# Forget rows and state-space rows fetched by DMA broadcast instead of by matrix products, the time steps computed beside the first merge, token blocks weighed together

## Chip, cores and metric

The kernel runs on one core of a Trainium2 chip. The metric is the device time of one execution in microseconds (us). A core has TensorE (PE, matrix products into eight PSUM banks), VectorE (DVE), ScalarE (ACT), GpSimd (POOL) and SyncE (SP). Nearly all DMAs of this kernel are issued from SP's program, in its order, so a wait in it holds back every transfer behind it.

## The reference, cut to what matters

The program computes two transformer-like blocks over 512 tokens of width 1024. The change touches the mixer of the first block: attention with a forget gate, and a state-space mixer (SSM) with 32 heads.

```python
proj = h @ w_in
q, k, v, f_raw, u_pool, z, xbc, dt_raw, gate_raw = split_columns(proj)
log_f = jax.nn.log_sigmoid(f_raw.astype(jnp.float32) + b_forget)     # 16 heads
...
F = jnp.transpose(jnp.cumsum(log_f, axis=1), (0, 2, 1))
logits = einsum(q, k) * scale + F[:, :, s0:s1, None] - F[:, :, None, :s1]
p = jax.nn.softmax(jnp.where(mask, logits, -jnp.inf), axis=-1)       # causal, blocks of 128 queries
...
dt = jax.nn.softplus(dt_raw.astype(f32) + dt_bias)                   # 32 heads
a = -jnp.exp(a_log.astype(f32))
a_cs = jnp.cumsum(dt * a, axis=2)                                    # within a chunk
seg = a_cs[:, :, :, None] - a_cs[:, :, None, :]
decay = jnp.where(causal, jnp.exp(jnp.where(causal, seg, 0.0)), 0.0)
scores = cb[..., None] * decay * dt[:, :, None]
y_diag = einsum(scores, xs);  y_off = einsum(cm, h_prev) * jnp.exp(a_cs)
y = (y_diag + y_off + d_skip * xs) * jax.nn.silu(z)                  # then an RMS norm by group
merged = gates[0] * y_att + gates[1] * y_pool + gates[2] * y_ssm
```

The term of F at the query drops out of the softmax, so the kernel needs only the row of F over the keys, the same for every query, which means the same on all 128 partitions.

## The kernel before

The mixer runs in stages with a barrier between them: opening (0 to 60 us), attention, first merge, pool, SSM, second merge. Inside a stage every engine follows its own program, and semaphores tie them. Products with fp32 weights are done in three passes: a weight is split by ACT (`high`) and DVE (`low`) into two fp32r parts, and PE multiplies high by high, high by low and low by high. A tile of 128 output columns is thus 24 matmuls of 512 columns.

**Opening.** The last product (L326) gives the raw forget gates, 128 columns of `w_in` of which 16 are used, and the first pair's queries.

**Attention** (`attention_stage`). Eight head pairs i, four query blocks b of 128. In a step (i, b) PE issues `scores(i, b+1)`, half a projection of the next pair (12 matmuls, L840), `turn` (transposes of the probabilities, L878), the other half, and `weigh` (L890). `scores` first spreads the forget row of each of the two heads over the partitions by two matmuls (L861: a picked column of 16 rows, broadcast, times the high and low part of F, at least 256 columns wide), then adds the products of queries and keys (L865). DVE takes `row_max` (L1034, adding `wide_mask`), `normalise`, the `low` parts of later weights, and six to eight steps of a matrix-vector product for the second block (`matvec`, L1067 and L1069), whose 1 MB strips SP loads into three slots. ACT does the exponents (L963) and the copies.

**First merge** (`merge_stage`, branch 0). Eight halves of weights, 48 matmuls each, on PE (L543); ACT and DVE prepare the next half (L517, L521) and apply the gate.

**SSM** (`ssm_stage`). First tiles: one for the 32 raw time steps (`dt`), then six of group 0, which pass a convolution (`conv` on DVE, L1578 and L1580) and an activation (tanh on ACT, `silu` on DVE, L1596). Between them DVE computes the time steps, softplus and the running sums `acs` (`raw_times` to `sums`, L1621 to L1650). `turn_small` needs them. Then for each of four groups i: tiles of the next group and gate tiles at ten places (`tile_at(i, 0)` to `(i, 9)`), `turn_x` for four token blocks (L1297), on DVE `weigh` for each (L1670, L1675), `chunk_products` (L1304), `state` (L1315), then four head pairs f: `rows` (L1330: each head's row of `acs` spread over the partitions by two matmuls of 512 columns), `exponents` on ACT (L1478 to L1482), `scores` on DVE (L1700, L1702), `heads` on PE (L1345, L1349), `outputs` on DVE (L1707, L1709), `square` on ACT.

The order of work is written out by hand; the lines below set it around the change. `more(i, n)` names the tile at place n of group i; `tile(t)` on DVE forms what is due of the earlier tiles and then makes the low part of tile t+2, and on ACT it waits for tile t before it makes the high part of tile t+2.

## Time and profile before

| | us |
|---|---|
| median of three runs | 2770.69 |
| the runs | 2768.95 to 2771.82 |
| profiled execution | 2773.53 |
| its span, first to last instruction | 2771.7 |
| PE busy in the span | 2518.8 (91%) |
| DVE busy | 1763.2 (64%) |
| ACT busy | 1132.4 (41%) |
| mean granted TensorE clock | 0.941 |

The span lacks 1.8 us of the execution's own time. Busy times of a stage are read from stretches cut at the barriers: attention from 59.7 to 338.6 us, the first merge to 433.9, SSM from 538.5 to 907.2. A matmul of 512 columns shows a duration of 0.39 us, but the next starts some 0.24 us after it, so the cost of products is read from start to start.

### The profile page before, as it was taken

To read this page: it belongs to the slowest core of one execution; us is meant where nothing else is said; L and a number is where in the kernel's file an instruction comes from. 1 tells how busy PE (TensorE), PEld (TensorE's weight loads), DVE (VectorE), ACT (ScalarE), POOL (GpSimd) and SP (SyncE) were. 2 spreads that over 40 slices of the span, in tenths; PEclk is the share of its full clock that TensorE was granted. 3 is DMA by queue.
4 is the path that set the end of the run, shared out by engine and by line. 5 is a ranking of instruction groups with operands and counts; after the bars stand their busy time and mean duration, and the time that the engine had idled before them with its cause. 6 is when DMAs were issued, how large, how long until landed. Compare 5 with 4: busy or idle time off the path is not lost. (4 is left out here: it accounts for less than half of the span.)

```text
span 2771.7 us, 32845 instructions
## 1 busy us (share of the span) xinstructions
PE 2518.8 (91%) x12831; PEld 1984.4 (72%) x12831; DVE 1763.2 (64%) x2557; ACT 1132.4 (41%) x1635; POOL 45.1 (2%) x153
## 2 busy tenths in 40 slices
PE   7999799989999989599993898899997979899998
PEld 6666487677777777388882356688886977688886
DVE  5888724486776675689984465677766573642434
ACT  4444322135545324478873243531324144441323
POOL 0000001000000000100001000000000000000000
PEclk8999799999999998599996999999998889999998
DMA  6776637122221843699983112224333314223221
GB/s 232 237 236 227 215 126 273 54 76 61 69 54 61 306 149 76 247 376 417 418 353 151 50 50 69 76 99 152 111 102 108 87 25 167 76 96 102 91 92 31
DMA packets 293562, 415.68 MB, mean 150 GB/s; under 512 B 24906, under 2 KB 212797, under 8 KB 283552
## 3 DMA queue, kind: packets, MB, share of 16 engines
q1 hardware_dynamic: 285568, 383.69, 40.8%
q0 software_dynamic: 5392, 20.97, 1.9%
...
## 5 line engine op out<-in xcount | busy, mean ns | idle before, releaser
L3597 PE MATMUL banks<-big,late_parts 128*128 128x512 f32 x1920 | 443.4, 393 | 11.1 <-DVE late_parts L3770 7.3
L3597 PEld LDWEIGHTS banks<-big,late_parts 128*128 128x128 f32 x1920 | 363.5, 189 | 89.4 <-DVE late_parts L3770 7.5
L3597 PE MATMUL banks<-h_parts_second,late_parts 128*128 128x512 f32 x1440 | 332.6, 391 | 12.8 <-DVE h_parts_second L3794 12.8
L3597 PEld LDWEIGHTS banks<-h_parts_second,late_parts 128*128 128x128 f32 x1440 | 272.0, 189 | 70.9 <-issue 14.4
L3770 DVE TENSOR_TENSOR late_parts<-w_second,late_parts 128x2048 fp32r<-128x2048 f32 x69 | 158.1, 2292 | 218.8 <-ACT late_parts L3659 218.7
L2300 DVE TENSOR_TENSOR expert_parts<-w,expert_parts 128x2048 fp32r<-128x2048 f32 x102 | 233.1, 2289 | 29.1 <-ACT expert_parts L2296 28.7
L1270 PE MATMUL banks<-h_parts,ssm_parts 128*128 128x512 f32 x984 | 239.8, 401 | 6.6 <-DVE ssm_parts L1566 6.1
L3659 ACT ACTIVATE late_parts<-w_second 128x2048 fp32r<-128x2048 f32 x69 | 132.0, 1914 | 256.1 <-PE banks L3597 256.1
L1270 PEld LDWEIGHTS banks<-h_parts,ssm_parts 128*128 128x128 f32 x984 | 186.6, 192 | 53.9 <-DVE ssm_parts L1566 7.9
L2296 ACT ACTIVATE expert_parts<-w 128x2048 fp32r<-128x2048 f32 x102 | 194.7, 1916 | 64.1 <-PE banks L2307 64.1
L2307 PE MATMUL banks<-expert_parts,expert_xt 128*128 128x512 f32 x816 | 195.2, 399 | 6.0 <-DVE expert_xt L2824 6.0
L2307 PEld LDWEIGHTS banks<-expert_parts,expert_xt 128*128 128x128 f32 x816 | 155.8, 193 | 39.4 <-DVE expert_xt L2824 6.9
L543 PE MATMUL banks<-h_parts,front_parts 128*128 128x512 f32 x576 | 135.5, 398 | 8.6 <-DVE front_parts L521 6.5
L840 PE MATMUL banks<-h_parts,qkv_parts 128*128 128x512 f32 x552 | 139.2, 402 | 3.4 <-SPq L158 3.4
L543 PEld LDWEIGHTS banks<-h_parts,front_parts 128*128 128x128 f32 x576 | 110.3, 192 | 33.4 <-DVE front_parts L521 6.8
L1069 DVE SCALAR_TENSOR_TENSOR attention_mod_sum<-w,silu_c,attention_mod_sum 128x512 f32<-128x512 f32 x168 | 126.1, 751 | 5.1
L840 PEld LDWEIGHTS banks<-h_parts,qkv_parts 128*128 128x128 f32 x552 | 101.5, 190 | 35.3 <-issue 11.4
L3682 ACT ACTIVATE tail_r<-banks,cols 128x512 f32<-128x512 f32 x64 | 40.5, 685 | 201.3 <-PE banks L3597 201.3
L543 PE MATMUL banks<-h_parts,ssm_parts 128*128 128x512 f32 x480 | 111.5, 394 | 6.0 <-DVE h_parts L1941 3.1
L3803 DVE TENSOR_TENSOR tail_q<-tail_r 128x512 f32<-128x512 f32 x64 | 41.4, 688 | 114.3 <-ACT tail_r L3682 114.2
L543 PEld LDWEIGHTS banks<-h_parts,ssm_parts 128*128 128x128 f32 x480 | 91.0, 190 | 26.2 <-issue 3.9
L2307 PE MATMUL banks<-expert_parts,expert_ht 128*128 128x512 f32 x408 | 99.2, 400 | 4.5 <-DVE expert_ht L2829 4.5
...
## 6 DMA issues: line engine op xcount, KB each, us to landing
...
```

The source lines that it names most:

```text
L543: mm = pe.matmul(out, self.parts[:, n % 2, w, kk, f * P:(f + 1) * P], x[:, v, kk, :], start=(start and kk == 0 and j == 0), stop=(stop and ...
L840: mm = pe.matmul(ps[:, bank, :], parts[:, j, w, kk, :], k.hp[:, x, kk, :], start=(kk == 0 and n == 0), stop=(kk == KD - 1 and n == 2))
L1069: ins = dve.scalar_tensor_tensor(out=acc, in0=w, scalar=by, in1=acc, op0=ALU.mult, op1=ALU.add)
L1270: mm = pe.matmul(ps[:, t % 2, :], parts[:, t % SPLITS, w, kk, :], k.hp[:, x, kk, :], start=(kk == 0 and j == 0), stop=(kk == KD - 1 and j ...
L2296: act.activation(self.high_part(h), self.raw(h), ACT.Copy).then_inc(self.high_done, 1)
L2300: dve.tensor_tensor(self.low_part(h), self.raw(h), self.high_part(h).bitcast(F32), ALU.subtract).then_inc(self.low_done, 1)
L2307: mm = pe.matmul(out, x[:, v, first + kk, :], self.tile(h, w, kk), start=(start and kk == 0 and j == 0), stop=(stop and kk == KE - 1 and j ...
L3597: mm = pe.matmul(ps[:, bank(n, f), :], w_part(n, w)[:, kk, f * P:(f + 1) * P], x[:, v, kk, :], start=(first_chunk(n) and kk == 0 and j == ...
L3659: act.activation(w_part(n, 0), raw_half(k, n), ACT.Copy).then_inc(s["high_done"], 1)
L3682: act.activation(r[:, c % 2, :], ps[:, bank(n, c % HT), :], ACT.Relu, bias=k.cols[:, b1 + at:b1 + at + 1]).then_inc(s["relu_done"], 1)
L3770: dve.tensor_tensor(w_part(n, 1), raw_half(k, n), w_part(n, 0).bitcast(F32), ALU.subtract).then_inc(s["low_done"], 1)
L3803: dve.tensor_tensor(q[:, c % 2, :], r[:, c % 2, :], r[:, c % 2, :], ALU.mult).then_inc(s["squared"], 1)
```

## The change

**Forget row in attention.** `F` is no longer spread by PE. DVE forms the running sum (without the sign change), SP stores it to DRAM (`forget_store`, 16 rows) and loads each pair's two rows by a broadcast over 128 partitions into `f_rows` (512 KB, two slots). `row_max` adds this row instead of `wide_mask`, and PE adds the causal mask of the diagonal block by one 128-column product of an identity (`eye`) with `mask` for each head.

**Time steps.** The forget gate's product takes 32 columns of the forget gates and 32 of the time steps (64 instead of 128 weight columns, two DMAs of 128-byte runs). ACT copies the raw time steps out of PSUM and SP stores them. The whole chain up to `acs` stands in the first merge (`time_steps(n)` behind half n), and its results go through DRAM to the SSM stage, whose `dt` tile, chain and parts of `acs` are gone. `chunk_ends` stays there.

**SSM rows.** `rows` on PE is gone. SP loads the row of `acs` of each head by broadcast (256 KB) into one of four buffers, two heads at a time, when the exponents two pairs before are done. `exponents` reads them from SBUF. On DVE `weigh` runs for all four token blocks before the next convolution is formed, and `outputs(i, f-1)` stands ahead of `scores(i, f+1)`. At the stage's end the two halves of one product change places.

```diff
+    k.dt_store, k.dt_raw = (k.nc.dram_tensor(name, (G_SSM * R_SSM, T), F32, kind="Internal").ap() for name in ("dt_store", "dt_raw"))
+    k.acs_store = k.nc.dram_tensor("acs_store", (G_SSM * R_SSM, T), F32, kind="Internal").ap()
...
+            sp.dma_start(f_raw[:, :, 0:DT_ROW], columns(w_in, F0, DT_ROW)).then_inc(s["forget_loaded"], 16)
+            sp.dma_start(f_raw[:, :, DT_ROW:], columns(w_in, DT0, GATED - DT_ROW)).then_inc(s["forget_loaded"], 16)
...
+                        mm = pe.matmul(ps[0:n, bank, :], w[:, a, kk, :], k.hp[:, v, kk, :], start=(kk == 0 and j == 0),
...
+                src = k.forget_store[2 * i:2 * i + 2, :].rearrange("(o h) t -> o h t", o=1).to_broadcast([P, 2, T])
+                sp.dma_start(f_rows[:, i % 2], src).then_inc(s[f"f_loaded{i % 2}"], 16)
...
+            sp.wait_ge(s["dt_copied"], 1)
+            sp.dma_start(k.dt_raw, dt).then_inc(s["dt_stored"], 16)
+            sp.wait_ge(s["f_summed"], 1)
+            sp.dma_start(k.forget_store, f_sum).then_inc(s["f_stored"], 16)
+            sp.wait_ge(s["f_stored"], 16)
+            load_forget(0)
+            load_forget(1)
...
+                    if i >= 1 and i + 1 < pairs and j == MOD_SLOTS:
+                        sp.wait_ge(s["max_done"], UNITS * i)
+                        load_forget(i + 1)
...
+                    pe.matmul(ps[:, unit % 4, 0:n], qt[rows, i % 2, b * P:n], kt[rows, i % 2, 0:n], start=True, stop=False)
...
-                    for x in range(2):
-                        pe.matmul(ps[:, unit % 4, 0:wide], pick[:, 2 * i + hh:2 * i + hh + 1].to_broadcast([HEADS, P]),
-                                  f_parts[:, x, 0:wide], start=(x == 0), stop=False)
...
+                    pe.matmul(ps[:, unit % 4, b * P:n], eye[:], mask[:], start=False, stop=True).then_inc(s["scores_done"], 1)
...
+            act.activation(eye[:], k.ident[:], ACT.Copy).then_inc(s["mask_ready"], 1)
+            act.activation(mask[:], k.future_mask[:], ACT.Copy, scale=-1.0).then_inc(s["mask_ready"], 1)
+            act.activation(dt, ps[DT_ROW:GATED, 0, :], ACT.Copy).then_inc(s["dt_copied"], 1)
...
+                    if b == 0 and hh == 0:
+                        dve.wait_ge(s[f"f_loaded{i % 2}"], 16 * (i // 2 + 1))
                     dve.wait_ge(s["scores_done"], unit + 1)
-                    dve.tensor_tensor_reduce(out=ps[:, unit % 4, 0:n], in0=ps[:, unit % 4, 0:n], in1=wide_mask[:, T - n:T], scale=1.0,
+                    dve.tensor_tensor_reduce(out=ps[:, unit % 4, 0:n], in0=ps[:, unit % 4, 0:n], in1=f_rows[:, i % 2, hh, 0:n], scale=1.0,
...
-            dve.wait_ge(s["f_high"], 1)
-            dve.tensor_tensor(f_parts[:, 1], neg_f, f_parts[:, 0].bitcast(F32), ALU.subtract).then_inc(s["f_ready"], 1)
...
+            dve.tensor_tensor_scan(f_sum, ones, f_ln, 0.0, ALU.mult, ALU.add).then_inc(s["f_summed"], 1)
...
-    tiles = [("dt", 0, 0)] + [("conv", 0, c) for c in range(NC_SSM)]
+    tiles = [("conv", 0, c) for c in range(NC_SSM)]
...
+        row = sb("row", [P, DEEP - 1, T])
+        row = [row[:, h, :] for h in range(DEEP - 1)] + [flat[:, 3 * KD * STRIP - T:]]
...
+            def tiles_to(t):
+                while RAWS + loaded.at < min(t, TILES):
+                    sp.wait_ge(s["w_low"], loaded.at + 1)
+                    load_ssm(k, sp, RAWS + loaded.take())
+
+            def load_rows(n):
+                for head in (2 * n, 2 * n + 1):
+                    sp.dma_start(row[head % DEEP], k.acs_store[head:head + 1, :].to_broadcast([P, T])).then_inc(s[f"row_loaded{head % DEEP}"], 16)
+
+            sp.dma_start(dt, k.dt_store).then_inc(s["small_loaded"], 16)
+            sp.dma_start(acs, k.acs_store).then_inc(s["small_loaded"], 16)
+            tiles_to(FIRST + 2)
+            load_rows(0)
+            load_rows(1)
+            for i in range(G_SSM):
+                if i + 1 == G_SSM:
+                    tiles_to(TILES)
+                    sp.wait_ge(s["w_low"], TILES)
+                    halves.load(sp, base)
+                    halves.load(sp, base + 1)
+                for f in range(KG):
+                    n = KG * i + f
+                    if i + 1 < G_SSM:
+                        tiles_to(more(i, 3 + f) + 7)
+                    if n + 2 < KG * G_SSM:
+                        sp.wait_ge(s["seg_done"], 2 * n + 2)
+                        sp.wait_ge(s["row_exp"], 2 * n + 2)
+                        load_rows(n + 2)
...
+                pe.wait_ge(s["acs_ready"], TB)
...
-            def rows(i, f):
...
-                    for x in range(2):
-                        mm = pe.matmul(ps[:, 4 + h % 2, :], pick[:, head:head + 1].to_broadcast([NH, P]), acs_parts[:, x, :],
-                                       start=(x == 0), stop=(x == 1))
-                    mm.then_inc(s["row_done"], 1)
...
+                    if f == 0 and i == 0:
+                        pe.wait_ge(s["decay_done"], 2)
+                    elif f == 0:
+                        pe.wait_ge(s["std_done"], i)
...
+                    act.wait_ge(s[f"row_loaded{h % DEEP}"], 16 * (head // DEEP + 1))
                     if head >= DEEP:
...
+                        ins = act.activation(seg[:, h % DEEP, mine], row[h % DEEP][:, mine], ACT.Abs, bias=small[1][:, c, head:head + 1])
                     ins.then_inc(s["seg_done"], 1)
...
-                weigh(i, 0)
-                weigh(i, 1)
+                for c in range(TB):
+                    weigh(i, c)
                 if more(i, 2) is not None:
                     form(more(i, 2))
-                weigh(i, 2)
...
                         follow(TILES)
+                    if f >= 1:
+                        outputs(i, f - 1)
                     if f + 1 < KG:
                         scores(i, f + 1)
                     if i + 1 == G_SSM and f in (0, 3):
                         halves.low(dve, base + f // 3)
-                    if f >= 1:
-                        outputs(i, f - 1)
...
+                sp.wait_ge(s["dt_summed"], 1)
+                sp.dma_start(k.dt_store, dt).then_inc(s["dt_out"], 16)
+                sp.dma_start(k.acs_store, acs).then_inc(s["dt_out"], 16)
+                sp.wait_ge(s["dt_out"], 32)
...
+                    act.wait_ge(k.small_loaded, 32)
+                    act.activation(k.a_log[:], k.a_log[:], ACT.Exp).then_inc(s["dt_act"], 1)
+                    act.wait_ge(s["dt_step"], 3)
+                    act.activation(e, e, ACT.Exp).then_inc(s["dt_act"], 1)
+                if not last and n == 1:
+                    act.wait_ge(s["dt_step"], 4)
+                    act.activation(t2, t1, ACT.Ln).then_inc(s["dt_act"], 1)
...
+            def time_steps(n):
+                if n == 0:
+                    dve.wait_ge(s["dt_loaded"], 16)
+                    dve.wait_ge(k.small_loaded, 32)
+                    dt_step(dve.memset(ones, 1.0))
+                    dt_step(dve.tensor_scalar(dt, dt, k.dt_bias[:], None, ALU.add))
+                    dt_step(dve.scalar_tensor_tensor(out=e, in0=dt, scalar=-1.0, in1=dt, op0=ALU.mult, op1=ALU.min))
+                elif n == 1:
...
+                    dt_step(dve.tensor_tensor(t1, t1, acs, ALU.add))
+                    dt_step(dve.tensor_tensor(t2, t2, acs, ALU.add))
...
+                    for c in range(TB):
+                        mine = slice(c * P, (c + 1) * P)
+                        ins = dve.tensor_tensor_scan(acs[:, mine], ones[:, mine], t1[:, mine], 0.0, ALU.mult, ALU.add)
+                    ins.then_inc(s["dt_summed"], 1)
```

PE's program in attention, around the widest step of the first pair. `attention_pick` and `attention_f_parts` are the spread forget row, `attention_eye` and `attention_mask` the mask product; "x4" counts two heads and two parts. Before:

```order
L890 MATMUL banks<-merged,attention_v 64x128 x4
L861 MATMUL banks<-attention_f_parts,attention_pick 128x512 x4
L865 MATMUL banks<-attention_kt,attention_qt 128x512 x2
L840 MATMUL banks<-h_parts,qkv_parts 128x512 x12
L878 MATMUL banks<-ident,merged 128x128 x6
L840 MATMUL banks<-h_parts,qkv_parts 128x512 x12
```

After:

```order
L915 MATMUL banks<-merged,attention_v 64x128 x4
L888 MATMUL banks<-attention_kt,attention_qt 128x512 x2
L891 MATMUL banks<-attention_mask,attention_eye 128x128 x2
L869 MATMUL banks<-h_parts,qkv_parts 128x512 x12
L903 MATMUL banks<-ident,merged 128x128 x6
L869 MATMUL banks<-h_parts,qkv_parts 128x512 x12
```

The four row products ahead of the scores are gone, and two narrow products stand behind them.

PE's program in SSM, from the stage's start to the first heads. L1270 (L1309 after) are tiles, 24 matmuls each; L1281 and L1287 transposes of the small tensors and of b; `ssm_acs_parts,ssm_pick` the rows. Before:

```order
L1270 MATMUL banks<-h_parts,ssm_parts 128x512 x192
L1277 MATMUL banks<-ssm_parts_plain,ones 128x128
L1281 MATMUL banks<-ident,ssm_xbc 128x32 x8
L1287 MATMUL banks<-ident,ssm_parts_plain 128x128 x4
L1270 MATMUL banks<-h_parts,ssm_parts 128x512 x24
L1297 MATMUL banks<-ident,ssm_parts_plain 128x128 x8
L1270 MATMUL banks<-h_parts,ssm_parts 128x512 x24
L1297 MATMUL banks<-ident,ssm_parts_plain 128x128 x8
L1304 MATMUL banks<-ssm_parts_plain 128x128 x4
L1270 MATMUL banks<-h_parts,ssm_parts 128x512 x24
L1315 MATMUL banks<-w 128x512 x3
L1330 MATMUL banks<-ssm_acs_parts,ssm_pick 128x512 x4
L1270 MATMUL banks<-h_parts,ssm_parts 128x512 x24
```

After (L1366 are the heads):

```order
L1309 MATMUL banks<-h_parts,ssm_parts 128x512 x168
L1315 MATMUL banks<-ssm_parts_plain,ones 128x128
L1319 MATMUL banks<-ident,ssm_xbc 128x32 x8
L1325 MATMUL banks<-ident,ssm_parts_plain 128x128 x4
L1309 MATMUL banks<-h_parts,ssm_parts 128x512 x24
L1335 MATMUL banks<-ident,ssm_parts_plain 128x128 x8
L1309 MATMUL banks<-h_parts,ssm_parts 128x512 x24
L1335 MATMUL banks<-ident,ssm_parts_plain 128x128 x8
L1342 MATMUL banks<-ssm_parts_plain 128x128 x4
L1309 MATMUL banks<-h_parts,ssm_parts 128x512 x24
L1353 MATMUL banks<-w 128x512 x3
L1309 MATMUL banks<-h_parts,ssm_parts 128x512 x24
L1366 MATMUL banks<-x,w 64x128 x4
```

One tile of the first eight is gone, and the two groups of row products.

DVE's program in SSM, group 1, from the low part of a tile to the mask of the chunk products (L1679 before, L1658 after). L1670/L1675 (L1649/L1654) weigh one token block; L1578/L1580 (L1589/L1591) are a convolution. Before:

```order
L1566 TENSOR_TENSOR ssm_parts<-w,ssm_parts 128x1024
L1670 TENSOR_TENSOR w<-banks,ssm_small 128x512
L1675 TENSOR_TENSOR w<-w,ssm_parts_plain 128x512
L1670 TENSOR_TENSOR w<-banks,ssm_small 128x512
L1675 TENSOR_TENSOR w<-w,ssm_parts_plain 128x512
L1578 TENSOR_SCALAR ssm_parts_plain<-ssm_u,ssm_parts_plain 128x512
L1580 SCALAR_TENSOR_TENSOR ssm_parts_plain<-ssm_u,ssm_parts_plain 128x512 x3
L1670 TENSOR_TENSOR w<-banks,ssm_small 128x512
L1675 TENSOR_TENSOR w<-w,ssm_parts_plain 128x512
L1670 TENSOR_TENSOR w<-banks,ssm_small 128x512
L1596 SCALAR_TENSOR_TENSOR ssm_parts_plain<-w,ssm_parts_plain 128x512
L1566 TENSOR_TENSOR ssm_parts<-w,ssm_parts 128x1024
L1679 TENSOR_TENSOR w<-banks,ssm_parts_plain 128x512
```

After:

```order
L1577 TENSOR_TENSOR ssm_parts<-w,ssm_parts 128x1024
L1649 TENSOR_TENSOR w<-banks,x 128x512
L1654 TENSOR_TENSOR w<-w,ssm_parts_plain 128x512
L1649 TENSOR_TENSOR w<-banks,x 128x512
L1654 TENSOR_TENSOR w<-w,ssm_parts_plain 128x512
L1649 TENSOR_TENSOR w<-banks,x 128x512
L1654 TENSOR_TENSOR w<-w,ssm_parts_plain 128x512
L1649 TENSOR_TENSOR w<-banks,x 128x512
L1589 TENSOR_SCALAR ssm_parts_plain<-ssm_u,ssm_parts_plain 128x512
L1591 SCALAR_TENSOR_TENSOR ssm_parts_plain<-ssm_u,ssm_parts_plain 128x512 x3
L1607 SCALAR_TENSOR_TENSOR ssm_parts_plain<-w,ssm_parts_plain 128x512
L1577 TENSOR_TENSOR ssm_parts<-w,ssm_parts 128x1024
L1658 TENSOR_TENSOR w<-banks,ssm_parts_plain 128x512
```

The third and fourth block are weighed ahead of the convolution instead of behind it; nothing else is removed from this stretch.

## Rows read from the trace of the kernel before

**Rows 1.** Stretches by stage: attention, first merge, SSM; busy us by engine, clock, DMA
```profile
core 0: us, PE busy (x) PEld busy (x) DVE busy (x) ACT busy (x) POOL busy (x), PEclk, DMA share, GB/s
59.70:338.60 278.90, 249.83 (x1448) 177.38 (x1448) 225.28 (x486) 107.26 (x274) 1.44 (x6) 0.95 0.69 230
338.60:433.90 95.30, 88.99 (x384) 73.19 (x384) 30.58 (x25) 26.56 (x26) 0.00 (x0) 0.96 0.34 111
538.50:907.20 368.70, 345.43 (x1770) 265.78 (x1770) 265.08 (x369) 176.93 (x348) 0.56 (x4) 0.97 0.23 65
```
**Rows 2.** Stretches of attention: one middle head pair, and the last one
```profile
201.20:233.60 32.40, 30.90 (x185) 22.07 (x184) 27.92 (x61) 13.31 (x35) 0.00 (x0) 1.00 0.75 244
298.35:332.80 34.45, 21.21 (x133) 13.36 (x132) 30.00 (x68) 10.01 (x30) 0.00 (x0) 0.75 0.70 239
```
**Rows 3.** Timeline, a middle pair: start us, us, engine, line, operation, count, [idle before]
```profile
200.54 0.73 PE L861 MATMUL banks<-attention_f_parts,attention_pick 16*128 16x256 f32 x4
201.20 0.49 PE L865 MATMUL banks<-attention_kt,attention_qt 64*128 64x128 f32 x4
...
223.58 1.19 PE L861 MATMUL banks<-attention_f_parts,attention_pick 16*128 16x512 f32 x4
224.70 1.13 PE L865 MATMUL banks<-attention_kt,attention_qt 64*128 64x512 f32 x4
...
228.66 0.82 PE L878 MATMUL banks<-ident,merged 128*128 128x128 f32 x6
229.23 2.98 PE L840 MATMUL banks<-h_parts,qkv_parts 128*128 128x512 f32 x12
...
225.97 0.70 DVE L1034 CUSTOM_DVE_ANT_0 banks<-banks,attention_wide_mask 128x512 f32<-128x512 f32 x1 [1.64 <-PE banks L865]
```
**Rows 4.** Timeline, start of attention; and landing times of the broadcasts of L2360
```profile
70.45 1.21 DVE L1086 TENSOR_TENSOR_SCAN merged<-merged 16x512 f32<-16x512 f32 x1
78.44 0.29 DVE L1034 CUSTOM_DVE_ANT_0 banks<-banks,attention_wide_mask 128x128 f32<-128x128 f32 x1
...
L2360 SPq DMA_DIRECT2D routing_both_b<-mod_rows x2: 339/382/425, 1094.5 to 1094.9; - x2
DMA to landing us min/median/max: 4.0/4.7/5.4
```
**Rows 5.** Timeline and one stretch, start of SSM
```profile
541.00 39.94 PE L1270 MATMUL banks<-h_parts,ssm_parts 128*128 128x512 f32 x168 [4.35 <-DVE ssm_parts L1566]
582.71 5.75 PE L1270 MATMUL banks<-h_parts,ssm_parts 128*128 128x512 f32 x24 [1.76 <-DVE ssm_parts L1566]
592.37 0.76 PE L1277 MATMUL banks<-ssm_parts_plain,ones 32*128 32x128 f32 x2 [3.92 <-DVE ssm_parts_plain L1650]
...
594.63 7.78 PE L1270 MATMUL banks<-h_parts,ssm_parts 128*128 128x512 f32 x24
...
574.63 3.33 DVE L1636 RECIPROCAL ssm_xbc<-ssm_xbc 32x512 f32<-32x512 f32 x1
...
581.00:601.00 20.00, 14.38 (x57) 11.72 (x58) 18.57 (x32) 6.48 (x13) 0.00 (x0) 0.83 0.29 79
```
**Rows 6.** Timeline of PE, SSM group 1, chunk products to first heads
```profile
691.55 2.08 PE L1304 MATMUL banks<-ssm_xbc 128*128 128x128 f32 x8 [3.42 <-DVE w L1670]
693.28 6.31 PE L1270 MATMUL banks<-h_parts,ssm_parts 128*128 128x512 f32 x24
...
708.87 1.18 PE L1330 MATMUL banks<-ssm_acs_parts,ssm_pick 32*128 32x512 f32 x4
709.98 0.66 PE L1345 MATMUL banks<-x,w 128*64 128x128 f32 x8
```
**Rows 7.** Timeline of DVE, SSM group 1, first convolution to the scores' end
```profile
681.38 0.55 DVE L1578 TENSOR_SCALAR ssm_parts_plain<-ssm_parts_plain 128x512 f32<-128x512 f32 x1 [3.61 <-ACT ssm_parts_plain L1433]
...
700.77 1.23 DVE L1566 TENSOR_TENSOR ssm_parts<-w,ssm_parts 128x1024 fp32r<-128x1024 f32 x1 [0.87 <-ACT ssm_parts L1425]
...
707.60 0.56 DVE L1702 TENSOR_TENSOR x<-x,ssm_xbc 128x384 f32<-128x384 f32 x1
```
**Rows 8.** Groups by line, ACT's exponents in SSM: count, busy us, mean ns, idle before
```profile
L1478 ACT ACTIVATE x<-banks,ssm_small 128x128 f32<-128x128 f32 x128 | 36.9, 387 | 17.3 <-PE banks L1330 17.3
L1482 ACT ACTIVATE x<-x 128x512 f32<-128x512 f32 x32 | 21.7, 678 | 0.0
L1480 ACT ACTIVATE x<-banks 128x384 f32<-128x384 f32 x32 | 17.0, 530 | 0.0
```

214 lines of the change are left out of this document (80 added, 134 removed).

## The prediction, made before the changed kernel was run

> **What bounds the kernel now.** I read first the busy time of the engines by stage [rows 1]. The page's chain of waits names mostly the second half of the program, which the diff does not touch. What is to be seen: TensorE (PE) is busy for 249.8 of the attention stage's 278.9 us and for 345.4 of the state-space (SSM) stage's 368.7, at clocks of 0.95 and 0.97. VectorE (DVE) is second in both (225.3 and 265.1). In the first merge stage DVE is busy for only 30.6 of 95.3. So what leaves PE in the two long stages is worth its time until DVE becomes the limit, and work put on DVE in the merge stage has room. The stages meet at barriers, so their gains add.
>
> How much PE can shrink is asked in the small. A middle head pair of attention takes 32.40 us with DVE busy 27.92; the last pair, which has no projections beside it, takes 34.45 with DVE busy 30.00 and PE at clock 0.75 [rows 2]. In SSM the timeline of one group decides, below.
>
> **Attention.** Each head's forget row is now spread over the partitions by four matmuls in a step (two heads, high and low part). They take, from their start to the start of the next row, 0.66 us at width 256 and 1.12 at 512 [rows 3]; width 256 comes twice, and 384 lies between at 0.88. A pair pays 2 x 0.66 + 0.88 + 1.12 = 3.3 us. In their place come two 128-column mask products in each step. None like them (fp32r, 128 columns) is in the trace. The nearest are the 128-column transposes: six from 228.66 to 229.23, 0.095 us each. From below the bound is 0.07, a quarter of the 1.12/4 of a row product four times as wide; from above 0.28, the score products of L865 at 512 columns, four in 1.13 [rows 3]. I take 0.1, near the transposes, which have this very shape: 0.8 us a pair, bounds 0.6 and 2.2. Gross that is 2.5 us a pair.
>
> DVE's work stays: the row maximum has the same shape with another second operand. DVE now waits 1.64 us for the scores of the widest step [rows 3], and some 3.8 in a pair (32.40 less 27.92, less small gaps). A pair can thus shrink to about 28.6 + what order costs; walking one pair through both engines gives 30.1, where DVE has just caught up. I take 2.3 us for each of six middle pairs, 2 for the first, 1.7 for the last (its last rows stand ahead of a DVE wait): 17.5 us.
>
> Against it stands a longer way for the rows. The scan ends at 71.66 [rows 4]. Then SP stores 32 KB, waits, and loads 512 KB by broadcast. A load of just this kind is in the trace, 512 KB broadcast from one DRAM row: 4.0 us to landing, 5.4 for a second behind it [rows 4]. The store I bound by the same 4.0. The first maximum could start at 71.7 + 4 + 4 = 79.7, against 78.44 now [rows 4]. PE reaches the turn of the first probabilities some 1.3 us after they are ready, so it loses about 1 us (0 to 3, as the three 1 MB strips issued ahead may hold the store back). SP is blocked meanwhile, and the third pair's weights are queued behind; ScalarE (ACT) wants them only after 85. Later row loads wait for a maximum that is past. They add 0.5 MB to some 7.9 MB a pair with the DMA share at 0.75 [rows 2]. Nothing.
>
> The Trainium skill, "DMA: Bandwidth & Descriptors", section "Latency and other measured facts", gives about 2 us as a DMA's fixed cost. By it the rows would be there near 77, and the 1 us would vanish. The trace shows 4.0 for the load, and I go by that.
>
> Attention: -17.5 + 1 = **-16.5 us**.
>
> **Opening and first merge.** The time steps' columns ride in the forget gate's product: same number of matmuls, same moving width, no time. The gate's weights come in 128-byte runs; nothing waits there for several us. The chain of the time steps (one reciprocal of 3.33 us [rows 5], some twelve short operations, four scans, about 13 us) goes into 65 us of DVE idleness, always behind the halves that PE needs. ACT gets two or three table loads, behind its halves as well. The final stores end the SP program near the stage's end. I take 0, with 2 us as the bound above.
>
> **SSM, first group.** Now: eight tiles of 5.7 us, the last of the first seven ending at 580.9, then waits of 1.76 and 3.92 us for DVE, and the small transposes only at 592.37; the tile after them takes 7.78 us, not 5.7, with the granted clock at 0.83 over 581 to 601, that is, partly at 1.2 instead of 2.4 GHz [rows 5]. After: one tile fewer and no chain on DVE, so they stand at 541.0 + 7 x 5.66 = 580.7. That is 11.7 us, plus 2 for the clock: 13.7. Further on the removed row products give 2.2 us ahead of the first heads. But the change also weighs all four token blocks first, and blocks 2 and 3 can only be weighed when PE is through another tile; the convolution (2.9 us) that DVE did in that gap now comes behind it. I make DVE late for the first heads by 2.4 us and the clock dip 1.2. With the two other row products, 2.2, the group gains about **15 us**.
>
> **SSM, groups 1 and 2.** Here lies the step that I most rest on. PE has two stretches to save: the wait of 3.42 us before the chunk products with the slow 2.08 and 6.31 us behind it (together some 5), and four row products at 1.11 [rows 6]: 9.4 us. But DVE works from 681.38 to 708.07 with hardly a gap [rows 7]: nothing of that is removed, only reordered. Without the one wait for ACT in it (0.87 us) scores of head pair 0 end at about 707, and PE, which would be there by 703.5, stalls 3.4 us in front of the heads, where now it stalls before the chunk products. The heads start at 707 against 709.98 [rows 6], and the slow stretch behind a stall moves along. After that a step of head pairs falls from 8.46 to 7.33 us (a tile 5.66, heads 1.68), which ACT and DVE can hold: ACT's three kinds of exponent work no longer wait for rows (17.3 us of waits) and are busy for 75.6/32 = 2.4 us a head, 4.7 a step [rows 8]. At the last heads I get **3.7 us** for each of the two groups.
>
> The Trainium skill, "TensorE: Matmul & The Clock Gate", section "HAM oscillation — how this bites in real kernels", warns that waits between bursts make the array restart slowly again and again. Read for this change, a rule against counting removed matmuls one for one. By it the price of a stall is the stall and the slow stretch behind it, here 3.4 + 1.5 us; if DVE let the stall vanish, both would be gained, which is rival 1. The trace agrees with the rule in kind [rows 6].
>
> **SSM, last group.** Fewer tiles, DVE has waits of its own there, four row products 4.5 us, of which 0.6 goes to the later mask: **3.9 us**. Each is carried to the end of the stage, where PE's products stand in line.
>
> Broadcast rows in SSM: two of 256 KB a step, the DMA share there being 0.23 [rows 1], issued when the exponents of one pair are done and wanted two steps on, so some 2 x 7.33 - 4.7 = 10 us ahead. At 4.0 to 5.4 us hidden.
>
> **Sum.** 16.5 + 0 + 15 + 2 x 3.7 + 3.9 = 42.8 us. The profiled execution took 2773.53 us (span 2771.7 and 1.8 around it), 2.8 above the median of 2770.69. So 2773.5 - 42.8 = 2730.7 for one like it, and 2770.7 - 42.8 = **2727.9** as a median; I say 2728.
>
> **Rivals.**
> 1. *PE alone is the limit.* DVE hides better than I walked it. Then SSM gives one tile 5.7, rows 16 x 1.12 = 17.9, waits 1.8 + 3.9 + 1.3 + 3.4 + 3.4, slow stretches 5: 42; attention 8 x 2.5 = 20 less 1. Together 61, 2710. For it: DVE's share is below PE's everywhere. Against: the gapless 27 us [rows 7].
> 2. *Attention gives little.* Mask products at 0.2 us cost 6 more, the first rows come at 82 (2 more), DVE, 27.9 of then 30, is late at the wide steps (3 more); SSM reaches 21 as the moved convolution delays all groups. 5.5 + 21 = 26.5: 2744.
> 3. *Slower: row loads set the pace.* With two sets of row buffers a step can't be shorter than (L + 4.7)/2, L being the landing time. From L = 12.2 a step is no shorter than now; to lose also the rest, 16 steps have to grow by 2.7 us over 7.33, L = 15.4. At L = 20 a step is 12.35 us, the kernel 2728 + 16 x 5.0 = 2808. The measured 4.0 to 5.4 speaks against, but four readers a step of one line of DRAM beside weight loads is not in the trace.
> 4. *It doesn't do what it says*: the stall merely moves in all groups and attention keeps its period, DVE-bound. Only one tile and the start of SSM are left, 11.7, and the merge costs 2 and the start 3: 2764; with other small losses no change.
>
> **Chances.** Forecast 0.57 (own range 2718 to 2738), rival 1 0.13, rival 2 0.20, rival 3 0.05, rival 4 0.05 (three fifths of it within 0.2%, which is 5.5 us and about what a measurement of this kernel can tell from no change). So faster 0.92, same 0.03, slower 0.05. The range reaches from near rival 1 over all of rival 2: 2711 to 2749.
>
> **What would show it.** Attention: periods of about 30.1 us between the first scores of pairs, two L891 products at some 0.2 us. Start: first row maximum near 79.7. SSM: small transposes some 11 to 12 us earlier in the stage; a stall of PE of 3 us before the heads of groups 1 and 2 that ends with DVE's scores, none before the chunk products; steps of 7.3 us. I am wrong if ACT waits for row loads, if DVE waits for strips or rows in attention beyond the first, or if the stages outside move by more than 2 us.

## The result, and the profile of the changed kernel

The changed kernel takes 2724.39 us (median), the kernel before 2770.49 us beside it: ratio 0.9825, 95% interval 0.9813 to 0.9838, 46.1 us less. One of the four executions of e10 below was a slow one (4254.99 us at a granted clock of 0.552), and its time is given as the median of the other three. The profiled execution has a span of 2722.5 us against 2771.7. Four rows of PE's timeline mark its stages (start, duration, line, operation, count, idle time before): the first projection of attention, the first product of the first merge, the first tile of the state-space (SSM) stage and the first product behind it.

```profile
60.66 12.81 PE L869 MATMUL banks<-h_parts,qkv_parts 128*128 128x512 f32 x48 [3.48 <-SPq L158]
...
324.04 21.15 PE L551 MATMUL banks<-h_parts,front_parts 128*128 128x512 f32 x84 [6.50 <-DVE front_parts L529]
...
522.26 39.97 PE L1309 MATMUL banks<-h_parts,ssm_parts 128*128 128x512 f32 x168 [4.35 <-DVE ssm_parts L1577]
...
859.86 23.65 PE L551 MATMUL banks<-h_parts,ssm_parts 128*128 128x512 f32 x96 [2.58 <-PEq L149]
```

The same four products stand at 62.89, 342.92, 541.00 and 907.26 in the trace of before:

| stretch, us | before | after | difference | predicted |
|---|---|---|---|---|
| up to the first projection | 62.89 | 60.66 | -2.2 | 0 |
| attention | 280.03 | 263.38 | -16.65 | -16.5 |
| first merge and pool | 198.08 | 198.22 | +0.1 | 0 |
| SSM | 366.26 | 337.60 | -28.7 | -26.3 |
| the rest | 1864.44 | 1862.64 | -1.8 | 0 |

The first and the last line are chance. The kernels below leave both stretches as the change has them, and begin their first projection anywhere from 60.0 to 65.1 us and take 1859.8 to 1869.3 us for the rest. SSM, where it is untouched, takes 337.60 to 337.70 us in six traces. So below a stage is compared with a stage rather than a total with a total.

**Attention.** First the stretches that answer to [rows 2] (columns as in [rows 1]): three middle pairs, a seven-us piece of the second of them, and the last pair.

```profile
98.92:128.93 30.01, 28.46 (x178) 20.64 (x176) 27.54 (x60) 13.29 (x35) 0.00 (x0) 1.00 0.83 280
128.93:160.78 31.85, 30.08 (x179) 21.74 (x177) 28.22 (x62) 13.30 (x35) 0.00 (x0) 0.95 0.80 264
131.00:138.00 7.00, 5.97 (x36) 4.54 (x37) 6.79 (x12) 1.94 (x6) 0.00 (x0) 0.76 0.72 243
...
220.78:250.79 30.01, 28.47 (x178) 20.64 (x176) 27.87 (x60) 13.29 (x35) 0.00 (x0) 1.00 0.72 244
...
280.79:314.00 33.21, 21.56 (x130) 13.75 (x129) 30.06 (x68) 10.10 (x30) 0.00 (x0) 0.64 0.77 266
```

Five of six middle periods are 30.0 us, against 32.4; PE's busy time in one fell from 30.90 to 28.46 and its idle time stayed at 1.5. One period took 31.85: the clock fell to 0.76 there. Of the kernels below with untouched attention one (e2) shows such a period too and takes 263.35 us, the six others 260.9 to 261.7. Against the one trace of the kernel before, the undisturbed gain is thus 18.4 to 19.2 us, not the 16.65 of the table.

Now the timeline that answers to [rows 3] and [rows 4]: a step's scores and masks, then VectorE (DVE) at the start of the stage.

```profile
212.32 1.13 PE L888 MATMUL banks<-attention_kt,attention_qt 64*128 64x512 f32 x4
213.38 0.44 PE L891 MATMUL banks<-attention_mask,attention_eye 128*128 128x128 f32 x2
...
68.00 1.21 DVE L1111 TENSOR_TENSOR_SCAN merged<-merged 16x512 f32<-16x512 f32 x1
69.14 2.32 DVE L1051 TENSOR_TENSOR qkv_parts<-w,qkv_parts 128x1024 fp32r<-128x1024 f32 x2
75.08 1.23 DVE L1051 TENSOR_TENSOR qkv_parts<-w,qkv_parts 128x1024 fp32r<-128x1024 f32 x1 [3.62 <-ACT qkv_parts L969]
76.22 0.29 DVE L1061 CUSTOM_DVE_ANT_0 banks<-banks,attention_f_rows 128x128 f32<-128x128 f32 x1
```

The first maximum stands 15.56 us behind the first projection, before it was 15.55. In this execution DVE starts it as soon as its own low part is done and does not wait for the rows. That is not the rule: in ten of the thirteen traces of kernels with the change DVE waits for them, for 0.25 to 2.67 us. In e5, the same kernel once more, PE ran at clock 1.00 from the first projection on (here at 0.68 up to 66.0 us) and came to the first scores after 12.45 us instead of 14.09. DVE then waited for the rows:

```profile
78.21 0.30 DVE L1061 CUSTOM_DVE_ANT_0 banks<-banks,attention_f_rows 128x128 f32<-128x128 f32 x1 [2.23 <-DMA attention_f_rows<-forget_store]
```

**SSM.** PE's waits in the stage, summed by line and releaser (total us, times, longest):

```profile
PE banks L1366 <- DVE x L1681: 9.6, 3, 3.7
PE banks L1309 <- DVE ssm_parts L1577: 4.4, 1, 4.4
PE banks L1335 <- DVE ssm_xbc L1607: 2.6, 1, 2.6
...
PE banks L1342 <- DVE w L1649: 1.9, 4, 0.6
PE banks L1353 <- DVE w L1658: 1.2, 1, 1.2
```

Before, PE waited 8.5 us ahead of the chunk products and not at all for the heads. Now it is the other way round: 1.9 there, 9.6 at the heads (L1366). Group 1, to be laid beside [rows 5] to [rows 7]: the small transposes of group 0, then PE and DVE around the first heads of group 1.

```profile
562.15 0.48 PE L1315 MATMUL banks<-ssm_parts_plain,ones 32*128 32x128 f32 x2
...
653.82 1.16 PE L1342 MATMUL banks<-ssm_xbc 128*128 128x128 f32 x8 [0.60 <-DVE w L1649]
654.73 5.73 PE L1309 MATMUL banks<-h_parts,ssm_parts 128*128 128x512 f32 x24
...
672.15 0.70 PE L1366 MATMUL banks<-x,w 128*64 128x128 f32 x8 [3.65 <-DVE x L1681]
...
674.92 6.24 PE L1309 MATMUL banks<-h_parts,ssm_parts 128*128 128x512 f32 x24
682.76 5.75 PE L1309 MATMUL banks<-h_parts,ssm_parts 128*128 128x512 f32 x24
690.12 5.75 PE L1309 MATMUL banks<-h_parts,ssm_parts 128*128 128x512 f32 x24
...
661.48 0.54 DVE L1589 TENSOR_SCALAR ssm_parts_plain<-ssm_parts_plain 128x512 f32<-128x512 f32 x1
662.05 2.33 DVE L1591 SCALAR_TENSOR_TENSOR ssm_parts_plain<-ssm_parts_plain 128x512 f32<-128x512 f32 x3
...
671.45 0.56 DVE L1681 TENSOR_TENSOR x<-x,ssm_xbc 128x384 f32<-128x384 f32 x1
```

The small transposes come 39.89 us after the stage's first tile, before 51.37. The stall of 3.65 us ends with DVE's last score, and the first step behind it takes 8.93 us (slow heads, a tile of 6.24), the others 7.36. From the stage's first tile to the last heads of group 0 it is 95.13 us (before 111.30). From one group's last heads to the next's it is 78.41 and 78.40 for groups 1 and 2 (81.93, 82.00), and from those of group 2 to the end of the stage 85.66 (91.03).

### The profile page after: what moved, and what is told of

Same layout as the page of the kernel before. It is cut to its first block and busy times, and to the rows that moved or that the text cites. A ratio compares the mean times of both kernels' runs of the same rounds, so it can differ in the third digit from the quotient of the medians.

```text
span 2722.5 us, 32575 instructions
## 1 busy us (share of the span) xinstructions
PE 2475.7 (91%) x12679; PEld 1956.2 (72%) x12679; DVE 1757.0 (65%) x2552; ACT 1138.3 (42%) x1635; POOL 45.4 (2%) x153
## 5 line engine op out<-in xcount | busy, mean ns | idle before, releaser
L3619 PEld LDWEIGHTS banks<-h_parts_second,late_parts 128*128 128x128 f32 x1440 | 272.1, 189 | 70.9 <-issue 14.4
L1309 PE MATMUL banks<-h_parts,ssm_parts 128*128 128x512 f32 x960 | 232.9, 400 | 4.9 <-DVE ssm_parts L1577 4.4
L1309 PEld LDWEIGHTS banks<-h_parts,ssm_parts 128*128 128x128 f32 x960 | 180.6, 191 | 51.2 <-issue 9.4
L551 PEld LDWEIGHTS banks<-h_parts,front_parts 128*128 128x128 f32 x576 | 110.5, 192 | 33.3 <-DVE front_parts L529 6.8
```

What stands on the lines that cost most here:

```text
L551: mm = pe.matmul(out, self.parts[:, n % 2, w, kk, f * P:(f + 1) * P], x[:, v, kk, :], start=(start and kk == 0 and j == 0), stop=(stop and ...
L1309: mm = pe.matmul(ps[:, t % 2, :], parts[:, t % SPLITS, w, kk, :], k.hp[:, x, kk, :], start=(kk == 0 and j == 0), stop=(kk == KD - 1 and j ...
L3619: mm = pe.matmul(ps[:, bank(n, f), :], w_part(n, w)[:, kk, f * P:(f + 1) * P], x[:, v, kk, :], start=(first_chunk(n) and kk == 0 and j == ...
```

## Experiments

All are edits of the changed kernel, and compute the same as it; added products are overwritten or read by nobody. On the chips of the experiments the kernel before took 2771.3 to 2773.5 us, so a ratio to it compares them; e5 is the changed kernel once more.

**e5, the base.** 

> The changed kernel itself, as the base for the three others of this call on the same chip: 2724 to 2727 us.

2726.10 us, ratio 0.9839 (0.9819 to 0.9858). Attention 261.18, SSM 337.69.

**e1, the order of weighing.**

```
-                for c in range(TB):
-                    weigh(i, c)
+                weigh(i, 0)
+                weigh(i, 1)
                 if more(i, 2) is not None:
                     form(more(i, 2))
+                weigh(i, 2)
+                weigh(i, 3)
```

> The changed kernel (2724.4 us), with the inputs of token blocks 0 and 1 weighed, then the convolution, then blocks 2 and 3, as before the change. Theory of the prediction: in groups 1 and 2 DVE is gapless up to the first scores whatever the order, so the heads start where they start now (669.5 + 2.6 in group 1); PE's stall of 3.65 us before the heads shrinks and one of about 3 us comes back before the chunk products. 2722 to 2728, group 0 may even gain up to 2 us, as the convolution fills DVE's wait of 1.75 us. Rival, PE's waits simply add: four groups lose 2.9 us of convolution and a slow stretch of 1.5 each, with no stall taken away behind: 2740 or more.

2727.07 us, ratio 0.9842 (0.9825 to 0.9860); SSM 339.61, 2.0 more than the changed kernel. The stall moves back, as said:

```profile
651.95 2.08 PE L1342 MATMUL banks<-ssm_xbc 128*128 128x128 f32 x8 [3.42 <-DVE w L1649]
653.68 7.80 PE L1309 MATMUL banks<-h_parts,ssm_parts 128*128 128x512 f32 x24
...
669.92 0.66 PE L1366 MATMUL banks<-x,w 128*64 128x128 f32 x8 [0.40 <-DVE x L1681]
```

I had expected the heads of group 1 to stay where they were; they start 1.2 us later in the stage. Group 0 takes 1.2 us less than in the changed kernel, the others 1.8, 0.5 and 1.0 us more. PE's waits at the chunk products and the heads together are 11.4 us against 11.5. So the reordering moves a stall and takes none away; its 2 us are in the slow stretches, among them that of the last group, on which more below. The totals do not show them.

**e2, PE's time in SSM put back.** Four 32-row products where a pair's row products stood; nobody reads their bank.

```
+            def rows(i, f):
...
+                for h in range(2):
+                    for x in range(2):
+                        pe.matmul(ps[:, 5, :], k.hp[0:NH, x, 0, 0:P], k.hp[0:NH, x, 1, :], start=(x == 0), stop=(x == 1))
...
+                rows(i, 0)
                 for f in range(KG):
                     tile_at(i, 4 + f)
+                    if f + 1 < KG:
+                        rows(i, f + 1)
                     heads(i, f)
```

> The changed kernel with the time of the removed row products put back on PE in the state-space stage: four 32-row products, 512 columns wide, where a head pair's row products stood, into a bank that nobody reads; the rows still come by DMA. Theory of the prediction: what the removal gave was PE's time, less what falls into the stalls before the heads. The first one of groups 0, 1 and 2 goes into stalls of 2.33, 3.65 and 3.64 us and costs nothing, the other 13 cost 1.11 us each: 14.4, so 2739. Rival 1, PE alone is the limit: 16 x 1.11 = 17.8, 2742. Rival 3, what counted was ScalarE's wait for the rows in PSUM, not PE's time: DVE and ACT hide most, below 2731.

2739.61 us, ratio 0.9880 (0.9863 to 0.9896), but SSM only 345.63 in its trace: 8.0 us more, not 14.4 (its opening and its rest happened to be 4.5 and 5.9 us longer than those of the changed kernel). Against the changed kernel the groups take 0.7, 2.2, 0.6 and 4.6 us more. The total lies on the expected 2739 by luck. The last group, which has no stall at its heads, pays its four products in full. In the others the products fill the stall, in group 0 wholly. In groups 1 and 2 the same stall is left, 1.19 and 1.20 us, but only behind that of group 1 is there a slow stretch still (a step of 10.03 us; 8.47 in group 2):

```profile
677.38 1.12 PE L1373 MATMUL banks<-x,w 128*64 128x128 f32 x8 [1.19 <-DVE x L1694]
...
757.94 0.66 PE L1373 MATMUL banks<-x,w 128*64 128x128 f32 x8 [1.20 <-DVE x L1694]
```

My expectation credited the stall with one product a group. It should have credited what the stall shrinks by and, where it goes, the slow stretch: 4.4 - 2.4 - 1.6 = 0.4 in group 2 (0.6 measured), 4.4 - 2.5 = 1.9 in group 1 (2.2 measured). Why the stretch stays in one group and goes in the other is open.

**e11, the order of outputs and scores.**

```
-                    if f >= 1:
-                        outputs(i, f - 1)
                     if f + 1 < KG:
                         scores(i, f + 1)
                     if i + 1 == G_SSM and f in (0, 3):
                         halves.low(dve, base + f // 3)
+                    if f >= 1:
+                        outputs(i, f - 1)
```

> The changed kernel (2726.1 us on the chip of e5) with scores ahead of outputs again in each step of DVE in the state-space stage, as before the change. Theory: DVE has 1.26 and 0.41 us of waits in a step of 7.36 and neither is waited for; within 2 us of the changed kernel, 2724 to 2728. Rival, the outputs free the bank of the heads two steps on, and their delay of 2.4 us holds PE up in every step: 3 steps in each of four groups at 0.5 to 1 us, 2732 to 2738.

2735.33 us, ratio 0.9869 (0.9852 to 0.9885); SSM 344.05, 6.4 us more. My theory of it fell. Scores wait for ScalarE's (ACT's) exponents, and outputs queued behind them come too late for the heads two steps on, whose bank they free (DVE, then PE):

```profile
697.11 0.56 DVE L1681 TENSOR_TENSOR x<-x,ssm_xbc 128x384 f32<-128x384 f32 x1
698.48 0.69 DVE L1679 TENSOR_TENSOR x<-x,w 128x512 f32<-128x512 f32 x1 [0.82 <-ACT x L1504]
...
701.21 0.66 PE L1366 MATMUL banks<-x,w 128*64 128x128 f32 x8 [1.32 <-DVE ys_plain L1688]
703.17 5.68 PE L1309 MATMUL banks<-h_parts,ssm_parts 128*128 128x512 f32 x24 [0.21 <-DVE ys_plain L1598]
```

The second and third steps of groups 0 and 1 take 8.19 and 9.01 us instead of 7.36. In the kernel before, the row products stood in that time. The groups take 2.3, 2.7, 1.2 and 0.2 us more than in the changed kernel.

**e12, the room of the row loads.**

```
                         sp.wait_ge(s["row_exp"], 2 * n + 2)
+                        sp.wait_ge(s["y_done"], n + 1)
                         load_rows(n + 2)
```

> The changed kernel (2726.1 us beside a kernel before of 2772.0) with the row loads of the state-space stage issued later: those of the pair after next wait for the heads' products of this pair too, and not only for its exponents. In the changed kernel's trace the rows of pairs 2 and 3 of group 1 are issued 15.6 and 11.2 us before the first exponent that reads them; so they would be issued about 7 us before it, against a landing time of 3.1 to 8.6 us (median 4.6). Theory (the loads are hidden with room to spare): within 2 us of the changed kernel, 2724 to 2728, no wait of ScalarE for a row beyond a single late one. Rival 3 in small, four descriptors on one line of DRAM beside weight loads are late as soon as the room is cut: ScalarE waits for rows in most steps, 2732 or more.

2725.72 us, ratio 0.9837 (0.9821 to 0.9854); SSM 337.28. In group 1 the rows are issued 6.6 us before their first use, and the exponents have no wait for them. In the last group ACT waits for a row twice, one wait more than I had allowed:

```profile
823.01 1.28 ACT L1501 ACTIVATE x<-ssm_row,x 128x128 f32<-128x128 f32 x4 [2.98 <-DMA ssm_row<-acs_store]
...
830.21 1.28 ACT L1501 ACTIVATE x<-ssm_row,x 128x128 f32<-128x128 f32 x4 [1.88 <-DMA ssm_row<-acs_store]
```

PE's steps there stay at 7.36 us, so this costs no time. In the changed kernel ACT has no wait for a row at all. There the loads are hidden with room to spare; with this edit the room is nearly used up.

**e7, the price of a mask product.**

```
-                    pe.matmul(..., eye[:], mask[:], start=False, stop=True).then_inc(s["scores_done"], 1)
+                    pe.matmul(..., eye[:], mask[:], start=False, stop=False)
+                    pe.matmul(..., eye[:], mask[:], start=False, stop=True).then_inc(s["scores_done"], 1)
```

> The changed kernel with every mask product made twice. Theory: PE is the limit in the pairs and a pair of mask products costs from its start to the next product's start 0.28 us, as in the trace of the changed kernel, so four steps cost 1.1 us a pair, periods of 31.1 us and 2733 us. It prices the disputed term of the sum. Rival, they cost as much as the 0.44 us that a row of two shows: 1.8 us a pair, 2739. Rival, DVE sets the period and they cost nothing: 2726.

2735.54 us, ratio 0.9865 (0.9849 to 0.9882). Periods are 30.76 us, 0.76 more for eight products: 0.095 us each; attention 267.28, 6.1 more (the rest of the 9.4 over e5 lies outside the stage).

```profile
226.69 0.28 PE L892 MATMUL banks<-attention_mask,attention_eye 128*128 128x128 f32 x1
226.80 0.27 PE L891 MATMUL banks<-attention_mask,attention_eye 128*128 128x128 f32 x1
```

A further one starts 0.11 us after the last. The 0.28 from the start of a pair to the next product is more than two such, but the twelve products behind it take 0.08 us less than before (2.88 against 2.96 to the next row, behind the scores of 256 columns). That this is a changeover which PE makes anyway is my reading.

**e3 and e6, PE's time in attention put back.** Two 16-row products for each head. In e3 they stand ahead of each head's score product, in e6 all four ahead of both:

```
+                    for x in range(2):
+                        pe.matmul(ps[:, unit % 4, 0:wide], k.hp[0:HEADS, x, 0, 0:P], k.hp[0:HEADS, x, 1, 0:wide], start=(x == 0), stop=(x == 1))
```

> The changed kernel with the time of the removed row products put back on PE in the attention stage: two 16-row products for each head, 256 to 512 columns wide, ahead of the scores in the same bank, overwritten by them; the rows still come by DMA, and the mask products stay. Theory: PE is the limit in the pairs (28.45 us busy of 30.0) and DVE only follows; 3.3 us a pair come back, of which 0.5 may fall into the wait of 0.81 us for the normalised probabilities: periods of 32.8 to 33.3 us and 8 x 2.8 to 3.3, so 2747 to 2751. Rival, DVE (27.9 of 30.0) sets the period and PE has room: less than 1.5 us a pair, below 2736.

> As e3_att_work, but the four 16-row products of a step stand together ahead of the score products of both heads, where the removed row products stood; so the two heads' score products follow each other again. Theory: e3 was slow because it parted the two heads' score products, which run side by side when adjacent (1.05 us for the four passes of both at 512 columns, and 1.05 us for the two passes of one head when parted), and because the clock fell behind that. With them together only the 3.3 us of PE time a pair come back: periods of 32.8 to 33.3 us, 8 x 2.8 to 3.3 more than the changed kernel, 2747 to 2751. Rival, any extra narrow work on PE here brings the clock down: periods of 36 us or more and above 2775. Rival, DVE sets the period: below 2736.

e3: 2807.34 us, ratio 1.0116 (1.0093 to 1.0139), slower than the kernel before and far outside what I expected. Its edit did more than add products: it also parted the score products of the two heads.

```profile
178.65 1.12 PE L891 MATMUL banks<-attention_kt,attention_qt 64*128 64x512 f32 x2
179.70 0.73 PE L890 MATMUL banks<-h_parts 16*128 16x512 f32 x2
```

Alone one head's two passes take 1.05 us to the next start; in the changed kernel both heads' four take 1.06 (212.32 to 213.38 above). They use different halves of the partitions, and cost together what one costs alone when adjacent. The Trainium skill, "TensorEngine Tiling (Array Packing)", section "Theoretical Speedup", gives up to twofold where one dimension of the product is at most 64; this trace agrees. Summed over the four widths the parting is worth some 2.9 us a period, an estimate from such starts in both traces. The periods are 40.2 and 41.7 us, at clocks of 0.92 and 0.88, against 33.3 at 1.00 in e6 below. So of the 6.9 to 8.4 us between them the larger part is the clock.

e6: 2761.32 us, ratio 0.9960 (0.9942 to 0.9977). Both theories hold in part: some periods are 33.3 us as expected, some 37.6, at a clock of 0.86.

```profile
170.70:204.00 33.30, 31.76 (x194) 23.00 (x193) 27.89 (x61) 13.31 (x35) 0.00 (x0) 1.00 0.76 252
204.00:241.61 37.61, 36.12 (x193) 26.16 (x193) 27.87 (x61) 13.41 (x35) 0.00 (x0) 0.86 0.68 224
```

**e10, the same time over all rows.** e6 with the operands over 128 rows instead of 16.

```
-                        pe.matmul(ps[:, unit % 4, 0:wide], k.hp[0:HEADS, x, 0, 0:P], k.hp[0:HEADS, x, 1, 0:wide], start=(x == 0), stop=(x == 1))
+                        pe.matmul(ps[:, unit % 4, 0:wide], k.hp[:, x, 0, 0:P], k.hp[:, x, 1, 0:wide], start=(x == 0), stop=(x == 1))
```

> e6_att_work_first with the added products over 128 rows in place of 16: same number, same columns, same time on PE. In e6 three of six periods took 37.6 us and not 33.3, with PE at the lower clock behind the waits of 0.81 and 0.69 us in each pair. Theory, products over few rows are what lets the clock fall behind so short a wait: all periods near 33.3 us, 2747 to 2752. Rival, it is the wait or the amount of short products, whatever their rows: as e6, 2753 to 2772, with periods of 37 us among them.

2749.15 us, ratio 0.9923 (0.9904 to 0.9943). All middle periods are 33.2 to 33.3 us; attention 286.34 against 304.61 in e6.

```profile
202.68 0.74 PE L890 MATMUL banks<-h_parts 128*128 128x256 f32 x4
...
203.34:236.59 33.25, 31.70 (x193) 22.96 (x192) 27.89 (x61) 13.31 (x35) 0.00 (x0) 1.00 0.77 254
236.59:269.87 33.28, 31.73 (x194) 22.98 (x193) 27.89 (x61) 13.31 (x35) 0.00 (x0) 1.00 0.61 206
```

Over the changed kernel that is 3.3 us a pair: PE's time in the pairs comes and goes whole.

**e4 and e8, a better order.** If the stall at the heads is DVE's, it must go when DVE does only there what the heads need. e4 puts two of the next group's convolutions behind later scores and the normalisations behind the first; e8 mends what e4's trace shows, and reorders the last group.

```
                 # e4, DVE; ACT's tanh of these tiles moves along
+                    if f == 1:
+                        ahead(conv, i, 2)
+                    if f == 2:
+                        ahead(silu, i, 1)
+                    if f == 3:
+                        ahead(conv, i, 3)
+                        ahead(silu, i, 2)
                 # e8
+                    if f == 2 and i + 1 < G_SSM:
+                        form(more(i, 6))
+                        ahead(conv, i, 2)
...
-                tile_at(i, 3)
                 states(i)
                 scores(i, 0)
+                tile_at(i, 3)
```

> The changed kernel with another order on DVE and ACT in groups 0 to 2 of the state-space stage: the convolutions of the next group's third and fourth tile stand behind the scores of head pairs 2 and 3 (their tanh on ACT moves along), and all four normalisations behind the scores of pair 0, where two stood ahead. Nothing is added or removed. Theory of the prediction (the stall before the heads is DVE's gapless work, and 3.4 + 1.4 us of it is not needed there): the stalls of 2.33, 3.65 and 3.64 us go, and with them the slow stretches behind (1.1 to 1.5 us each): 3.4 + 5 + 5 = 13, so 2711. Rival, the work is only moved and DVE is late by as much at head pairs 1 to 3 (DVE has 1.8 us of waits in a step of 7.36): gain of at most 4 us, 2720 to 2724. Worse than 2726 if ACT's order now holds PE up.

> e4_conv_late mended where its trace shows new stalls: on DVE the gate of the second gate tile ahead of the postponed convolution (1.2 us a group), the tile's low part behind the scores of pair 0 (0.4 us a group); on ACT the postponed tanh behind the gate's (0.7 us a group); in the last group the last silu ahead of the tile's parts (2.6 us), the mask ahead of gate and low part (0.6 to 1.2 us) and the normalisations behind the gate (0.75 us). Theory (PE waits only for what DVE and ACT do too early, there is enough room in both): the stage shrinks from 337.6 to 319 to 323 us, so 15 to 18 us under the changed kernel: 2707 to 2711. Rival, each stall only moves on to the next product, as DVE has little more to give: no better than e4_conv_late, 2718 to 2722.

e4: 2719.62 us, ratio 0.9819 (0.9798 to 0.9841); SSM 331.56, 6 us less, not 13. The stalls at the heads fell to 0.4 us, but the postponed convolution stood ahead of a gate (1.20 us of wait for PE in each group) and ACT's tanh ahead of another (0.69). Its four times scatter from 2713 to 2728 us, so the gain is read from the stage and not from the total.

e8: 2709.77 us, ratio 0.9778 (0.9761 to 0.9794), 16 us under e5 on the same chip; SSM 322.50, as expected. PE's waits there:

```profile
PE banks L1310 <- DVE ssm_parts L1590: 4.3, 1, 4.3
PE banks L1343 <- DVE w L1670: 1.9, 4, 0.6
PE banks L1367 <- DVE x L1702: 1.3, 3, 0.4
PE banks L1336 <- ACT w L1494: 0.8, 1, 0.8
```

It has the lowest time here together with e9, 0.6% under the changed kernel.

**e9, the last wait in a pair.** e8, and PE makes the next pair's second scores between the turn and the weighing of the last probabilities.

```
                     if i + 1 < pairs and b < 3:
                         project(i + 1, b, KD // 2, KD)
+                    elif i + 1 < pairs:
+                        scores(i + 1, 1)
                     weigh(i, b)
```

> e8_spread, and in attention PE makes the next pair's scores of block 1 between the turn of the last probabilities and their weighing, where it waits 0.74 us for ScalarE's copy in each pair (0.69 to 0.81 us more for VectorE stay). Nothing is added or removed. Theory (PE is the limit in the pairs, its waits are the only idle time): 0.74 us for each of seven pairs, periods of 29.3 us, 5 us less than e8_spread: 2703 to 2706. Rival, DVE (27.9 us busy) is late elsewhere as soon as PE asks earlier, and the wait moves: 2708 to 2711.

2710.49 us, ratio 0.9776 (0.9760 to 0.9792): no gain over e8. The wait of 0.74 us is gone, the period falls from 30.01 to 29.84 only. At the first half projection PE is 0.71 us ahead of e8, at the second only 0.16. It now arrives too early at what DVE has summed:

```profile
230.31 1.06 PE L923 MATMUL banks<-attention_mod_sum,ones 128*32 128x256 f32 x12 [0.16 <-DVE attention_mod_sum L1098]
```

The rival held. In e8 and in e9 DVE ends this sum 8.2 us behind the start of the period, and the row maxima and the next turn wait for it. So at 30 us DVE's order is the next limit of a pair, with DVE busy for 27.9.

## Why the prediction was right, and where it was not

**Right as a whole.** 2728 was predicted, 2724.4 came; the interval of the ratio leaves 45 to 52 us of gain, and 42.8 were forecast, slightly too little. Nearly all of it came from the two stages that were named (16.65 and 28.7 us). In attention the sum is nearer to the measured gain than its terms are; in SSM it is 2.4 us short.

**Attention, periods.** 30.1 predicted, 30.0 measured. The row products' 3.3 us and the mask products' 0.1 us each hold: e7 gives 0.095, and 3.3 - 8 x 0.1 = 2.5 is close to the 2.44 us by which PE's busy time fell. The deduction for DVE was needed less than I made it (2.4 came, not 2.3), but e9 shows that DVE is the next limit.

**Attention, the ends.** The first pair gave 2.28 us (2 predicted), the last 1.3 (1.7), at a clock of 0.64 against 0.75. The first scores came 0.65 us earlier in the stage, where I had put +1 us for the rows' way. In the profiled execution that loss is absent. The store landed after 2.9 us, not the 4.0 that I bounded it by; the first load after 4.0. The rows were there at about 76.1, 6.9 us behind the scan's end instead of 8, when DVE had just come to want them. In other executions the term is there: the first maximum stands 7.7 us behind the scan's end in e5, 7.8 in e11 and 8.0 in e1, and the first pair takes 25.39 us in e5 and 25.83 in e11, 1.2 and 1.6 more than the 24.2 of the others with untouched attention. So +1 was a fair mean of two cases, none and 1.2 to 1.6. The rule of the Trainium skill that I weighed ("DMA: Bandwidth & Descriptors", section "Latency and other measured facts"), about 2 us, is below both the store (2.9 us here, 4.0 in e1) and the load (4.0).

**Attention, the sum.** That 16.65 lies on the predicted 16.5 is luck. It is 0.65 + 2.28 + 12.4 + 1.3: six middle periods gave 12.4 us instead of 13.8, as one ran slow by 1.85, and the missing +1 made up for it. Undisturbed, the stage gives 18.4 to 19.2 us.

**Opening and merge.** 198.08 and 198.22 us: nothing, as said, though DVE is busy for 41.8 us in the merge where it was for 30.6.

**SSM, group 0.** It gave 16.2 us against 15; the terms that I listed add up to 14.5. The small transposes came 11.48 us earlier (11.7), PE's stall at the heads was 2.33 us (2.4), with a slow stretch of 1.6 us behind it (1.2). By these the gain would be smaller, not larger. What I left out are two terms of 1.0 us each: the wait ahead of the chunk products fell from 1.32 to 0.34 us, and from the small transposes to the next tile it is 1.29 us instead of 2.26.

```profile
610.95 1.16 PE L1304 MATMUL banks<-ssm_parts_plain 128*128 128x128 f32 x8 [1.32 <-DVE w L1670]
...
576.73 1.16 PE L1342 MATMUL banks<-ssm_parts_plain 128*128 128x128 f32 x8 [0.34 <-DVE w L1649]
```

**SSM, groups 1 and 2.** 3.5 and 3.6 us against 3.7, and by the mechanism: no stall ahead of the chunk products (0.6), one of 3.65 (3.4) at the heads that ends with DVE's scores, steps of 7.36 (7.33). e1 shows that the stall only moves; e4 and e8 show that it goes with another order of DVE's work (with ACT's tanh moved along). But one step of the working was hollow. "A step falls to 7.33 us, which ACT and DVE can hold" counted busy times. It holds only because the change also puts outputs ahead of scores, and I gave that edit no price at all. Without it (e11) the stage loses 6.4 us and steps of groups 0 to 2 grow to 8.2 to 9.0. Of the 3.5 us that group 1 gained 2.7 go again, in group 2 1.2 of 3.6. That the total came out right hides it.

**The worth of the row products.** The sixteen removed sets are 17.8 us of PE's time; put back into the changed kernel (e2) they cost 8.0, and the two orders undone 6.4 and 2.0. With the 11.5 of the earlier start that is 27.9 of 28.7. The parts are not independent, so this sum is a check and no proof; the kernel with both order and products undone was not run.

**Last group.** It gave 5.4 us against 3.9. The term was too small by 1.5: before, PE ran at 0.83 from 842 to 850 us, behind the stall of 2.63 us; in the changed kernel it ran at 1.00 behind the same stall. In e1 that stretch is slow again (a tile of 7.23 us), and in the nine other traces that have this stall it is fast. So it is slow in just the two traces with the old order of weighing. With one trace of each it is not shown whether the order does it or chance.

**Row loads and rivals.** In group 1 the rows are issued 11 to 15.6 us ahead (10 predicted), and they land in 3.1 to 8.6 us over the stage. e12 cuts the room to 6.6 us without loss of time, though ACT then waits twice. Rival 3 is out. Rival 1 is as well: PE still waits 9.6 us at the heads. Rival 2's mask price (0.2) is refuted by e7. Its row time (82) was not reached in any trace: the first maximum stood at 76.2 to 81.2 us. Rival 4 is out by the gains of both stages.
